# Order of the products in the opening steps, and the constant matmuls at stage borders

## The reference

```
x += 1/2 * rms(SwiGLU_1(rms(x)))                           feed-forward, width 2816
x += rms(W_out [GLA | DiffAttn | Retention](rms(x) @ W_in))   mixer
x += 1/2 * rms(SwiGLU_2(rms(x)))                           feed-forward
rms(v) = v * rsqrt(mean(v*v) + 1e-6) * gain
```

## Time and profile before

| | us |
|---|---|
| median of 3 runs | 1359.73 |
| lowest, highest | 1357.12, 1360.03 |
| profiled execution, span from first to last instruction | 1357.8 |
| profiled execution, time around the span | not given |
| PE busy | 1333.1 |
| DVE busy | 811.5 |
| ACT busy | 635.9 |
| granted TensorE clock, mean of the span | 0.997 |

### The profile page before, as it was taken

One profiled execution on the slowest core, in us unless ns is written; L12 is line 12 of the kernel. 1 busy time (PEld: TensorE's weight loads), 2 busy tenths in 40 slices (PEclk: granted clock), 3 DMA queues, 4 the chain that ended last, 5 costly groups with the idle time before them and its releaser, 6 DMA issues.

```text
span 1357.8 us, 24700 instructions
## 1 busy us (share of the span) xinstructions
PE 1333.1 (98%) x9613; PEld 1294.5 (95%) x9613; DVE 811.5 (60%) x1230; ACT 635.9 (47%) x1001; POOL 128.4 (9%) x135
## 2 busy tenths in 40 slices
PE   6999999999999999999999999999999999999998
PEld 5999999998889999999999999999888899999998
DVE  5755544686676855554486555438866677555532
ACT  4544433554456644443464443437435565444433
POOL 2000000451000300000030000004500020000000
PEclk9999999999999999999999999999999999999999
DMA  6555554543344445545545544555333345554552
GB/s 182 170 170 169 158 169 145 152 131 97 82 132 112 122 146 148 154 139 147 157 121 148 154 143 144 154 149 158 101 85 88 100 125 159 151 153 144 146 150 66
DMA packets 351753, 187.42 MB, mean 138 GB/s; under 512 B 6320, under 2 KB 348620, under 8 KB 351688
## 3 DMA queue, kind: packets, MB, share of 16 engines
q1 hardware_dynamic: 348368, 177.49, 45.9%
q0 software_dynamic: 2480, 8.03, 1.7%
q10 hardware_dynamic: 840, 0.99, 0.3%
HBM read 182.17 MB, written 4.33 MB: 137 GB/s over the span
## 4 chain that ended last, share of the span: by engine, by line
PE 94%; DVE 3%; DMA 1%; ACT 1%; issue 1%; DVEq 0%; ACTq 0%; POOL 0%; SPq 0%; POOLq 0%
PE ps L637 29%; PE ps L638 28%; PE ps L639 28%; DVE w_l L514 1%; PE ps L832 1%; PE ps L933 1%; DMA raw<-in_ffn_w_up_dram 1%; PE ps L807 1%; PE ps L946 1%; PE ps L905 0%; DMA par_in<-in_ret_norm_dram 0%; DVE y L1326 0%; PE ps L690 0%; PE ps L911 0%; PE ps L682 0%
## 5 line engine op out<-in xcount | busy, mean ns | idle before, releaser
L637 PE MATMUL ps<-xn_l,w_h 128*128 128x320 f32 x1840 | 580.8, 316 | 2.6 <-DVE xn_l L1315 2.6
L638 PE MATMUL ps<-xn_h,w_l 128*128 128x320 f32 x1840 | 569.3, 309 | 0.0
L639 PE MATMUL ps<-xn_h,w_h 128*128 128x320 f32 x1840 | 569.1, 309 | 0.0
L514 DVE TENSOR_TENSOR w_l<-raw,w_h 128x1024 fp32r<-128x1024 f32 (+1 forms) x340 | 408.0, 1204 | 169.5 <-ACT w_h L505 169.3
L505 ACT ACTIVATE w_h<-raw 128x1024 fp32r<-128x1024 f32 (+1 forms) x342 | 352.8, 1036 | 225.0 <-DMA raw<-in_ffn_w_down_dram 128.2
L637 PEld LDWEIGHTS ps<-xn_l,w_h 128*128 128x128 f32 x1840 | 346.1, 188 | 13.3 <-issue 5.0
L638 PEld LDWEIGHTS ps<-xn_h,w_l 128*128 128x128 f32 x1840 | 346.4, 188 | 1.5
L639 PEld LDWEIGHTS ps<-xn_h,w_h 128*128 128x128 f32 x1840 | 346.3, 188 | 0.0
L637 PE MATMUL ps<-hid_l,w_h 128*128 128x320 f32 x704 | 217.6, 309 | 0.0
L638 PE MATMUL ps<-hid_h,w_l 128*128 128x320 f32 x704 | 217.5, 309 | 0.0
L639 PE MATMUL ps<-hid_h,w_h 128*128 128x320 f32 x704 | 217.5, 309 | 0.0
(11 more groups left out here) (243 smaller groups left out, 1131.3 us busy)
## 6 DMA issues: line engine op xcount, KB each, us to landing
raw<-in_ffn_w_up_dram SPq DMA_DIRECT2D x176, 512.0 KB, 3.8
raw<-in_ffn_w_down_dram SPq DMA_DIRECT2D x64, 448.0 KB, 3.8
raw<-in_w_in_dram SPq DMA_DIRECT2D x54, 512.0 KB, 3.8
raw<-in_ffn_w_down_dram SPq DMA_DIRECT2D x32, 512.0 KB, 4.1
raw<-in_w_out_dram SPq DMA_DIRECT2D x16, 512.0 KB, 4.2
const<-in_tables_dram POOLq DMA_DIRECT2D x8, 298.0 KB, 4.4
x_in<-in_x_prompt_dram SPq DMA_DIRECT2D x1, 1024.0 KB, 6.4
scores<-in_cache_diff_k_dram POOLq DMA_DIRECT2D x2, 512.0 KB, 5.4
```

The lines of the kernel that those rows point to most:

```text
L514: dve.tensor_tensor(w_l[s][:, 0:cols], raw[s][:, 0:cols], w_h[s][:, 0:cols], ALU.subtract).then_inc(w_lo, 1)
L637: pe.matmul(out, w_h[s][:, w], xl, start=first, stop=False)
L638: pe.matmul(out, w_l[s][:, w], xh, start=False, stop=False)
L639: return pe.matmul(out, w_h[s][:, w], xh, start=False, stop=last)
```

## The change

Three edits:

- `opening_step` waits for the high part of the block first and issues two matmuls per unit with it (`w_l` and `w_h` with `xh`). Then it waits for the low part and issues the third (`w_h` with `xl`) for each unit. This holds for blocks 0 to 3 of every opening and for all eight blocks of the output projection. `product` and the second half of the opening stay as they are.
- A feed-forward that isn't the last ends with `keep_busy_hidden()` instead of `keep_busy(6)`: twelve single pass matmuls of the hidden activations' high part, which nobody reads: four of 512 columns, four of 256, four of 320 with 64 weight columns.
- After the mixer `keep_busy(4)` stands for `keep_busy(6)`.

```diff
             def opening_step(l, u0, n, i, order=range(KD), xh=xn_h, xl=xn_l):
 
-                pe.wait_ge(xn_lo, (l * 4 + n) * KD + i + 1)
+                k = order[i]
+                w = slice(k * P, k * P + P)
+                pe.wait_ge(xn_hi, (l * 4 + n) * KD + i + 1)
                 for t in range(OPENING):
                     if i == 0:
                         pe.wait_ge(w_lo, l * UNITS + u0 + t + 1)
-                    tile_part(slot(l, u0 + t), t, i, i + 1, order, xh, xl)
+                    out, s = ps[:, t, 0:T], slot(l, u0 + t)
+                    pe.matmul(out, w_l[s][:, w], xh[:, k, :], start=i == 0, stop=False)
+                    pe.matmul(out, w_h[s][:, w], xh[:, k, :], start=False, stop=False)
+                pe.wait_ge(xn_lo, (l * 4 + n) * KD + i + 1)
+                for t in range(OPENING):
+                    s = slot(l, u0 + t)
+                    mm = pe.matmul(ps[:, t, 0:T], w_h[s][:, w], xl[:, k, :], start=False, stop=i == KD - 1)
+                    if i == KD - 1:
+                        mm.then_inc(w_used, 1)
...
+            def keep_busy_hidden():
+
+                flat = hid_h[:, 4:6, :].rearrange("p k t -> p (k t)")
+                for m, n in ((P, 512), (P, 256), (64, T)):
+                    for k in range(4):
+                        pe.matmul(ps_stat[0:m, 0:n], hid_h[:, k % 2, 0:m], flat[:, 0:n], start=True, stop=True, skip_group_check=True)
...
                     spread(l, norm // 2)
-                    keep_busy(6)
+                    keep_busy_hidden()
...
                 spread(l, 1)
-                keep_busy(6)
+                keep_busy(4)
                 ffn(l, U_F2, G_F2, 4, 3, 2)
```

## The result

The changed kernel takes 1361.91 us (median of 11 runs, 1359.76 to 1363.56) against 1359.78 of the kernel before in the same comparison (11 runs): ratio 1.0017, interval 1.0009 to 1.0024. It is slower by 2.1 us, where 1.8 us less was forecast, and lies outside the range. Measured once more on another chip it was 1.0019 (1.0010 to 1.0027).

What follows compares the result with a forecast made beforehand. TensorE, its matmuls busy 98% of the span, was taken to bound the kernel. Terms 2.2 + 0.2 - 0.1 - 0.44 gave 1.8 us less than 1359.7: 1357.9 us, range 1355.0 to 1361.0.

Steps and rivals of the forecast that it cites:

- Steps 1 to 3: Borders after feed-forwards: opening starts earlier on the high part, shorter filling, then a wait for the last xn_l; 0.72 us gained each.
- step 2: Filling after a feed-forward: twelve single pass matmuls take 2.0 us against 2.76 busy before, so the opening starts 1.0 earlier.
- Step 4: Kernel's first opening: six matmuls instead of three remain behind the last weight, 0.44 us lost, 0.88 at low clock.
- Step 5: Output projection's last step frees slots 0.88 us later, delaying the sum of squares: 0.5 lost at second border, 0.85 at fifth.
- Step 6: Second and fifth borders, after the mixers: 0.72 gained each, less the new stalls, leaving +0.2 and -0.1 us.
- the sum: All gains and losses over the five borders and the first opening: 1.8 us less, 1357.9 us.
- rival B: Less filling lets the clock fall at all five borders, 1.1 us per fall: 2.6 slower, 1362.3 us; chance 0.10.

Runs made afterwards that it cites:

- order alone: Kernel before with only the new order in the opening steps, keeping the six old filling calls: 1362.37 us, ratio 1.0020.
- filling alone: Kernel before with only the shorter filling, the opening in its old order: 1358.41 us, ratio 0.9986.

## Why the prediction was wrong, by its steps

**Steps 1 to 3** were right in place and size: opening at 2.74 to 2.78 behind the spread (2.8), a gap in front of the last xn_l of 0.26 (0.29), a gain of 0.73 per border (0.72). They hold only where the clock doesn't fall. Nothing was lost into the mixers. One size in step 2 was off: the six old calls take 2.41 us and not 2.76 (order alone). So the shorter filling lets the opening start 0.44 earlier than the old one would, not 0.76, and is worth 0.20 of the 0.73.

**Step 4**, the first opening, was mis-sized. Its mechanism was right, six matmuls instead of three behind the last weight. I put down 0.44 and kept 0.88 as the upper end for the low clock. It is 0.41 where the clock stays full; that the one pair of profiles has 0.87 is luck. Over the profiles it is 1.3 in the mean, and alone the edit costs 2.1 us (median against median), most of it with a lower clock. I asked only at which clock the three matmuls run, not whether the early, broken start changes the clock.

**Step 5** was right: the square of tile 0 starts 0.88 later against its step, the new waits are 0.49 (0.5 forecast) and 1.27 (0.61 + 0.85 = 1.46 forecast). The fifth border's wait varies from execution to execution: 0.10 to 1.07 in the eight profiles with the old order in the output projection, 1.27 to 1.62 in the five with the new, 0.93 more in the mean. What I didn't see is that such a wait stands in the very stretch behind which the clock falls. With the wait for inv filled, falls stayed at just the two borders where such a wait stands (0.35 and 1.62). That it brings more falls while the wait for inv is open is not shown: in the ten profiles with that wait open, the clock fell at 5 of 14 borders that had a wait for the sum of squares and at 20 of 36 that had none, and the run with the old order in the output projection doesn't settle it.

**Step 6 and the sum** are where the forecast broke. The price of a fall was right: at the second border, with a fall in either profile, the stat of x stands 16.51 behind the spread instead of 17.37, a gain of 0.86 (0.9 forecast), and a fall of the usual length costs 1.0 to 1.2 (16.50 to 16.67 instead of 15.48). The shorter filling under the old order made it 0.41; the new order gives that up. What failed is that the sum counts one fall at a border before and one after, and puts nothing down for further ones. There are more: mean clock 0.9926 and 0.9930 against 0.9973 to 0.9977. At 0.84 us per 0.001 that alone is some 3.5 to 4 us (what step 4 costs by the clock is in it), against 1.8 forecast as gain; the measured sum is +2.1. So at equal clock the forecast's 1.8 us are about there, and the falls take them twice over.

So **rival B** happened (falls at further borders), given 0.10, and with it the prediction's own sign of being wrong, falls at more than two borders. Its size was right, 1.1 per fall and decisive from two more on, though that its 1362.3 lies so near the 1361.9 is luck: it left out what the start adds. Its cause was not right: it blamed the shorter filling, and that alone makes the kernel faster. What spoke for a higher chance stood in the material: the three runs spread over 2.9 us, and one fall costs 1.1. I read that spread as noise of measurement. By the 33 later executions most of such a spread is the clock: from 1.000, no low stretch that the record has, to 0.993, about five of 3.4 us each (one lowers the mean by 0.0013). An edit that moves waits about could change the count.

The Trainium skill (TensorE: Matmul & The Clock Gate, section HAM oscillation) has waits between bursts bring the clock down. The traces agree that waits matter: the falls come around 1.5 us of one-column matmuls and a 0.47 us wait, and filling only that wait removed most of them. The waits of that section's example are for a DMA and several times longer than 0.47 us, so by its example alone no fall was due here.

**Open.** With the new order behind the borders alone the clock is 0.9955, with the filling alone 0.9981; the new order there adds no stall that I found ahead of the spread, and the falls of the variant lie where those of the others do. Why it has more of them, nothing here tells. How much of the changed kernel's extra falls the start and the output projection bring is known only roughly, from the three runs that change one of these places.

## What to carry to other kernels

When an effect is below half a per cent, take every execution's mean granted clock along with its time, and look whether the record of the clock reaches to the kernel's start; ask of each edit both its time at equal clock and what it does to the stretch in front of a fall. Fill TensorE's waits inside a stretch of narrow matmuls, not only what follows it. A reordering that moves a buffer's release counts that release's whole queue.

## What the hardware showed that I had not expected

Most of the difference between this kernel's executions goes with the clock: 1357.4 us at 1.000 and 1363.8 at 0.993. Four records of 128 columns in a 0.47 us wait take the mean clock from 0.9955 to 0.9978, for 2.1 us. And the price of a fall of the same 3.4 us ran from 0.41 to 1.70 us by what stood behind it: 0.41 with idle time behind a short filling, 1.16 in the kernel before, 1.70 with the old filling and the new order.
